# Two convolution feed-forward down projections by seven block products instead of eight

## The reference, cut to what matters

```python
def conv_ffn(h, w_up, conv_w, conv_b, w_down):
    u = h @ w_up                      # 1024 -> 2 * 2816
    # causal depthwise convolution of width 3 along the tokens, + conv_b
    ...
    a, gate = jnp.split(u, 2, axis=-1)
    return (jax.nn.silu(gate) * a) @ w_down   # 2816 -> 1024
...
        x = x + conv_ffn(h, ffn_w_up[layer], ffn_conv_w[layer], ffn_conv_b[layer],
                         ffn_w_down[layer])
```

## Time and profile before

| | us |
|---|---|
| median of 3 runs (3202.98 to 3204.32) | 3203.75 |
| span of the profiled execution | 3201.8 |
| lies around the span, median less span | 1.95 |
| PE busy | 3186.1 |
| DVE busy | 1969.6 |
| ACT busy | 1271.3 |
| POOL busy | 404.6 |

### The profile page before, as it was taken

How to read it: one execution, slowest core, us unless ns; L and a number is a source line. 1 busy time by engine, 2 the same in 40 slices (tenths; PEclk the granted TensorE clock), 3 DMA queues, 4 the chain that set the end, 5 groups by cost and what they waited for, 6 DMA issues and landing times.

```text
span 3201.8 us, 44978 instructions
## 1 busy us (share of the span) xinstructions
PE 3186.1 (100%) x16214; PEld 2672.4 (83%) x16214; DVE 1969.6 (62%) x2804; ACT 1271.3 (40%) x1734; POOL 404.6 (13%) x356
## 2 busy tenths in 40 slices
PE   9999999999999999999999999999999999999998
PEld 7788888889998788888889998768888888888887
DVE  8455567585557455557585555666665744585656
ACT  4433333334453433343334453254332523553423
POOL 2100000124221100000124221051000101320001
PEclk9999999999999999999999999999999999999999
...
GB/s 267 67 167 206 126 94 167 140 92 106 106 99 106 55 169 208 121 98 166 142 87 106 106 99 83 86 21 112 99 99 93 105 99 92 47 85 100 92 99 79
DMA packets 100037, 359.24 MB, mean 112 GB/s; under 512 B 11056, under 2 KB 13360, under 8 KB 99760
## 3 DMA queue, kind: packets, MB, share of 16 engines
...
...
## 4 chain that ended last, share of the span: by engine, by line
PE 94%; DVE 2%; POOLq 1%; issue 1%; ACT 1%; DVEq 1%; DMA 0%; ACTq 0%; SPq 0%; POOL 0%
PE pb L687 21%; PE pb L688 21%; PE pb L689 21%; PE pb L1002 6%; PE pb L719 2%; PE pb L720 2%; PE pb L723 2%; PE pb L759 2%; PE pb L757 2%; PE pb L758 2%; PE pb L1110 1%; PE pb L1485 1%; PE pb L1486 1%; PE pb L1487 1%; PE pb L978 1%
## 5 line engine op out<-in xcount | busy, mean ns | idle before, releaser
L1557 ACT ACTIVATE hi<-raw 128x1024 fp32r<-128x1024 f32 x500 | 524.8, 1056 | 850.0 <-PE pb L689 543.5
L2181 DVE TENSOR_TENSOR lo<-raw,hi 128x1024 fp32r<-128x1024 f32 (+1 forms) x500 | 617.6, 1241 | 330.1 <-ACT hi L1557 304.3
L687 PE MATMUL pb<-yH,hi 128*128 128x512 f32 (+1 forms) x1664 | 644.2, 387 | 0.0
L688 PE MATMUL pb<-yL,hi 128*128 128x512 f32 (+1 forms) x1664 | 644.0, 387 | 0.0
L689 PE MATMUL pb<-yH,lo 128*128 128x512 f32 (+1 forms) x1664 | 643.9, 387 | 0.0
L687 PE MATMUL pb<-hH,hi 128*128 128x512 f32 x1128 | 440.5, 391 | 0.0
L688 PE MATMUL pb<-hL,hi 128*128 128x512 f32 x1128 | 439.0, 389 | 0.0
L689 PE MATMUL pb<-hH,lo 128*128 128x512 f32 x1128 | 438.9, 389 | 0.0
L687 PEld LDWEIGHTS pb<-yH,hi 128*128 128x128 f32 x1664 | 312.5, 188 | 63.6
L689 PEld LDWEIGHTS pb<-yH,lo 128*128 128x128 f32 x1664 | 312.4, 188 | 63.5
L688 PEld LDWEIGHTS pb<-yL,hi 128*128 128x128 f32 x1664 | 312.5, 188 | 63.4
...
## 6 DMA issues: line engine op xcount, KB each, us to landing
...
```

Of the source, the lines that this page charges most:

```text
L687: pe.matmul(out, whi, ahi, start=first, stop=False)
L688: pe.matmul(out, whi, alo, start=False, stop=False)
L1557: act.activation(hi[:, s], raw[:, s], ACT.Copy).then_inc(hi_ready, 1)
L2181: dve.tensor_tensor(lo[:, s, 0:width], raw[:, s, 0:width], hi[:, s, 0:width].bitcast(F32), ALU.subtract).then_inc(lo_ready, 1)
```

## The change

The down projections of the first two slabs of each layer's convolution block, four in all, are done by seven products. A down slab becomes four groups g = 0 to 3 of two output tiles. Each group has 84 matmuls of 256 columns. The inner channels are split into even and odd hidden tiles (the weights are put into that order on the host), the tokens into halves. Products 0 to 6 of hidden tiles are numbered m; the pair (2k, 2k+1) gives four token sums t1 to t4. DVE makes them, ACT rounds them (`middle_hi`), DVE makes remainders (`middle_lo`, event `m_lo`). GpSimd makes the weight sums into a new buffer `ext` (even groups) or `act3` (odd groups), ACT and DVE split them (`down_sum_hi`, `down_sum_lo`, event `e_lo`). Results are added to `x` straight from the banks, in six adds for a group, and counted by `x_part`. Groups 0 and 1 are interleaved: `lead0`, `lead1`, `follow0`, `follow1`, then groups 2 and 3 whole. SP's loads of the tiles behind a group wait for that group's weight sums too. `zT` and `rows` change places, and the scratch for GpSimd's transfers is smaller.

```diff
+FAST_1 = 2 * len(FAST_SLABS) * FAST_GROUPS
+FAST_DOWN = (0, 1)
...
+        d_sum = lambda q: act3[:, 4:7] if q else ext[:, 0:3]
+        d_sumL = lambda q: halved[:, 4:7] if q else extR[:, 0:3]
+        d_sumH = lambda q: tabR[:, 1:4] if q else extR[:, 3:6]
+        d_even = act3[:, 7]
...
+            loaded = early
+            for layer in range(LAYERS):
+                for j in FAST_DOWN:
+                    n = d_tile(layer, j) + RING
+                    into_ring_from(loaded, n)
+                    for g in range(FAST_GROUPS):
+                        sp.wait_ge(w_sums, d_at(layer, j, g) + 1)
+                        into_ring(n + 2 * g)
+                        into_ring(n + 2 * g + 1)
+                    loaded = n + KT
+            into_ring_from(loaded, TILES)
...
+            def down_sums(layer, j, g):
+                e, at = d_sum(g % 2), d_at(layer, j, g)
+                four_sums(d_tile(layer, j) + 2 * g, [e[:, i] for i in range(3)],
+                          5 * (at - 1) + (2 if g == 2 else 0))
...
+                def product_of(out, weights, tokens, first=True, ks=range(4), rest=False):
+                    (wH, wL), (aH, aL) = weights, tokens
+                    for k in ks:
+                        w = slice(k * P, (k + 1) * P)
+                        for n, (wP, aP) in enumerate(((wH, aH), (wH, aL), (wL, aH))):
+                            ins = pe.matmul(out, wP[:, w], aP[:, k], start=first and k == n == 0, stop=k == 3 and n == 2,
+                                            skip_group_check=not first and not rest)
+                    return ins
...
+                def begin():
+                    pe.wait_ge(lo_ready, tiles.next())
+                    pe.wait_ge(bank_free, banks.next(2))
+                    if g == 0:
+                        pe.wait_ge(y_ready, y0 + 7)
+                    product_of(one_sum, own(s0, 0), middle(0, 0)).then_inc(p_full, 1)
+                def with_own_sum():
+                    pe.wait_ge(lo_ready, tiles.next())
+                    if g == 0:
+                        pe.wait_ge(m_lo, t_all - 1)
+                    product_of(other_sum, own(s1, 0), token(1)).then_inc(p_full, 1)
+                def lead():
+                    begin()
+                    with_own_sum()
+                    product_of(upper, own(s0, 1), middle(1, 0), ks=early)
+                    product_of(lower_sum, own(s1, 1), token(4), ks=early)
+                def follow():
+                    ks = range(4)
+                    pe.wait_ge(e_lo, at + 1)
+                    if g == 0:
+                        pe.wait_ge(x_part, 3 * (p0 - FAST_1) + 1)
+                        product_of(one_sum, summed_w(2), token(2), False, early)
+                        pe.wait_ge(y_ready, y0 + KT)
+                        ks = late
+                    product_of(upper, own(s0, 1), middle(1, 0), False, late, True).then_inc(tile_done, 1)
+                    pe.wait_ge(m_lo, t_all)
+                    product_of(lower_sum, own(s1, 1), token(4), False, late, True).then_inc(tile_done, 1)
+                    pe.wait_ge(x_part, 3 * (p0 - FAST_1) + (3 if g else 1))
+                    product_of(one_sum, summed_w(2), token(2), False, ks).then_inc(p_full, 1)
+                    pe.wait_ge(x_part, 3 * (p0 - FAST_1) + (4 if g else 2))
+                    product_of(other_sum, summed_w(4), middle(1, 1), False).then_inc(p_full, 1)
+                    pe.wait_ge(x_part, 3 * (p0 - FAST_1) + (6 if g else 5))
+                    product_of(one_sum, summed_w(3), token(3), False).then_inc(p_full, 1)
+                def whole():
+                    begin()
+                    product_of(upper, own(s0, 1), middle(1, 0)).then_inc(tile_done, 1)
+                    with_own_sum()
+                    if g == 2:
+                        product_of(lower_sum, own(s1, 1), token(4)).then_inc(tile_done, 1)
+                    pe.wait_ge(e_lo, at + 1)
+                    pe.wait_ge(x_part, 3 * (at - FAST_1) + 1)
+                    product_of(one_sum, summed_w(2), token(2), False).then_inc(p_full, 1)
+                    if g == 3:
+                        product_of(lower_sum, own(s1, 1), token(4)).then_inc(tile_done, 1)
+                    pe.wait_ge(x_part, 3 * (at - FAST_1) + 2)
+                    product_of(other_sum, summed_w(4), middle(1, 1), False).then_inc(p_full, 1)
+                    pe.wait_ge(x_part, 3 * (at - FAST_1) + 3)
+                    product_of(one_sum, summed_w(3), token(3), False).then_inc(p_full, 1)
+                return lead, follow, whole
...
+            def fast_down(layer, j, y0):
+                (lead0, follow0, _), (lead1, follow1, _) = (down_group(layer, j, g, y0) for g in (0, 1))
+                lead0()
+                lead1()
+                follow0()
+                follow1()
+                for g in (2, 3):
+                    down_group(layer, j, g, y0)[2]()
...
+                    if j in FAST_DOWN:
+                        fast_down(layer, j, y_k.value())
+                    elif last:
...
+                        if fast and i >= 2 * n - RING:
+                            if i < 2 * n - 1:
+                                down_hi(layer, j, (i - 2 * n + RING) // 2, i % 2)
+                            if i in (2 * n - 3, 2 * n - 2):
+                                down_sum_hi(layer, j, i - 2 * n + 3)
+                        elif i + 1 < 2 * n:
...
+                    if fast:
+                        product_rounded(n - 1)
+                        act.wait_ge(m_last, slab + 1)
+                        middle_hi(3, 1, 4)
+                        for g in (2, 3):
+                            down_hi(layer, j, g, 0)
+                            down_hi(layer, j, g, 1)
+                            down_sum_hi(layer, j, g)
+                        done.next(KT)
+                        for s in (1, 2, 3):
+                            tick(s)
...
+                def one_of():
+                    dve.wait_ge(p_full, p + first)
+                    dve.tensor_tensor(x0[:, TH[0]], X, x0[:, TH[0]], ALU.add).then_inc(x_part, 1)
...
+            def fast_down(layer, j, finish):
+                one0, other0, two0, lower0, upper0, last0 = x_adds(layer, j, 0)
+                one1, other1, two1, lower1, upper1, last1 = x_adds(layer, j, 1)
+                one0()
+                other0()
+                down_lo(layer, j, 1, 1)
+                finish()
+                one1()
+                other1()
+                middle_lo(3, 1, 4, 5 * (d_slab(layer, j) + 1))
+                down_sum_lo(layer, j, 1)
+                two0()
+                lower0()
+                down_lo(layer, j, 2, 0)
+                upper0()
+                last0()
+                two1()
+                lower1()
+                upper1()
+                down_lo(layer, j, 2, 1)
+                last1()
+                one, other, two, lower, upper, last = x_adds(layer, j, 2)
+                one()
+                down_lo(layer, j, 3, 0)
+                other()
+                down_sum_lo(layer, j, 2)
+                lower()
+                two()
+                down_lo(layer, j, 3, 1)
+                upper()
+                last()
+                one, other, two, lower, upper, last = x_adds(layer, j, 3)
+                one()
+                down_sum_lo(layer, j, 3)
+                tick(1)
+                other()
+                two()
+                tick(2)
+                lower()
+                upper()
+                tick(3)
+                last()
...
+                    def first_token_sum(k):
+                        ins = dve.tensor_tensor(d_raw(1, k), d_even[:, TH[1]], d_even[:, TH[0]], ALU.subtract)
+                        if k == 3:
+                            ins.then_inc(m_sums, 1)
+                    def token_sums_of(k, made):
+                        b1, b2 = d_even, A[:, 2]
+                        _, t2, t3, t4 = (d_raw(i, k) for i in (1, 2, 3, 4))
+                        dve.tensor_tensor(t3, b2[:, TH[1]], b1[:, TH[1]], ALU.subtract)
+                        dve.drain()
+                        dve.tensor_tensor(t2, t3, b1[:, TH[0]], ALU.add)
+                        dve.drain()
+                        dve.tensor_tensor(t4, b2[:, TH[0]], t2, ALU.subtract)
+                        dve.drain().then_inc(made, 1)
+                    def remainder(m):
+                        dve.wait_ge(product_hi, ph.next())
+                        dve.tensor_tensor(midL[:, m], product_at(m), midH[:, m].bitcast(F32), ALU.subtract)
+                        dve.drain().then_inc(y_ready, 1)
...
+                        if fast and i == 2 * n - 1:
+                            remainder(m - 1)
+                            middle_lo(3, 0, 1, 5 * slab + 4)
                         drained.next()
                         dve.wait_ge(tile_done, done.next())
                         dve.tensor_tensor(st[:, s], pb[:, s], rows, ALU.mult).then_inc(bank_free, 1)
```

(30 more changed lines are left out.)

154 lines of the change are left out of this document (127 added, 27 removed).

## The result

| | before | after |
|---|---|---|
| median, us | 3203.49 (3202.98 to 3204.32, 4 runs) | 3267.51 (3266.33 to 3268.15, 4 runs) |
| ratio, 95% interval | | 1.0199 (1.0185 to 1.0214) |
| span of the profiled execution | 3201.8 | 3265.9 |

What follows compares the result with a forecast made beforehand. PE's own work was taken as the bound (busy 3186.1 of 3201.8 us). Per slab -3.2 + 4.0 + 1.2 + 1.0 = +3.0, four slabs +12, so a median of some 3216, range 3202 to 3225.

Steps and rivals of the forecast that it cites:

- Term 1: Down slabs on PE: 336 matmuls of 256 columns replace 43.52 us of work, gaining 3.2 a slab, 12.8 for four.
- Term 2: First down matmul: PE waits for product 6's remainder, behind DVE's queue of the second-last up tile, 4.0 us (3.5 to 4.7).
- Rival D: Seam: GpSimd stretches DVE's taps by half, as remainders; first wait 5.0 to 5.5, kernel 3219 to 3227; chance 0.17.
- the token work of the first twelve up tiles: Up tiles ahead of the down stage: DVE's token work fits beside its 4.7 of 5.44 us, at no cost.
- Term 3: Group 2: PE waits for its weight sums, made by GpSimd only after group 0; 1.2 us a slab, bounds 0.9 to 2.4.
- Term 4: After the seam wait: PE's clock falls to half, 1.9 us of work hit, 1.0 lost a slab, bounds 0 to 1.7.
- The rest costs nothing: Down stage: DVE's group work takes 6.9 of 10.1 us, token work fits, loads run ahead; no added time.
- Sum: Per slab: -3.2 + 4.0 + 1.2 + 1.0 = +3.0 us; four slabs +12.
- B: Down slabs: both waits, but clock holds and GpSimd hardly disturbs DVE; +1.2 to +1.9 a slab, 3208 to 3212; chance 0.20.
- C: Seam: DVE isn't late, only the gain from removed matmuls is left, 3191 to 3197; chance 0.11.

Runs made afterwards that it cites:

- the last kernel: Only groups 2 and 3 by seven products, DVE's queue reordered, GpSimd's group 3 sums held back, against the kernel before: 3198.02, ratio 0.9983.

## Why the prediction was right, and where it failed

**Term 1, matmuls removed (12.8): consistent.** Rows show 0.120 from matmul to matmul after too, at the full clock; with this term, the waits and the loss worked out from the granted clock, the sum closes to 1 us, and the last kernel gets 5.3 of the 6.4 that half of it promises.

**Term 2, the wait for product 6 (4.0 a slab): the step that failed.** Place and mechanism were right, with DVE's queue of the second-last up tile read to the instruction: 3.5 forecast with GpSimd idle, 3.4 measured where nothing else disturbs it. Measured in all was 14.6 in a layer's first slab and 10.9 in its second. Two things were missing. First, GpSimd: the prediction took two rows in which remainders took half as much again for a rate, and let it act on few instructions, for 0.5. It is an added wait for the rest of the GpSimd instruction under way, on each DVE instruction with two SBUF inputs that begins in that time: 8.0 and 7.6. The rows already held it: 2.84 less 1.76 and 3.46 less 2.36 are both 1.1, where a rate would have given unequal differences. The first of these rows is one instruction and the second two, of which only one was hit: in the trace the two tiles' remainders take 1.22 and 2.32. Rival D had the place right, the taps suffer too, but it also took a rate, for 1.5 to 2 in place of 8. Second, the first slab: "the token work of the first twelve up tiles fits beside DVE's 4.7 of 5.44" is so for a DVE that starts on time. In a layer's first slab it starts behind PE; before, its shorter tiles had made that good by the eleventh, and with token sums they don't, which costs 3.3 (6.7 less 3.4, without GpSimd).

**Term 3, the second wait (1.2, bounds 0.9 to 2.4): 2.7.** The chain was right and mis-sized for the same reason: group 2's four sums take 6.5 (2314.08 to 2320.54) where 5.8 was forecast, the tile's remainder 1.54 where 1.15, and the sums' remainder 2.48 where 1.7. The lower bound was also added up wrongly: with the hand-overs at nothing the terms make 11.3, less 10.8 is 0.5, not 0.9.

**Term 4, the clock (1.0, bounds 0 to 1.7): 3.3 to 3.8.** The prediction put 1.9 us of work into the low stretch of each slab. Behind the first waits it was 2.9 to 5.5, which costs 2.0 and 1.3 in layer 0. And it didn't ask whether the second wait would bring the clock down again, which it did each time, for 3.4 us of work and a loss of 1.5.

**"The rest costs nothing": right for the waits it named.** No wait for `x_part`, `m_lo` or loads; the token work is the exception, and showed as more of term 2, as the prediction said it would.

**Sum.** A slab: -3.2 + 12.7 + 2.7 + 3.8 = +16.0, four times 64; the 3.8 holds the 3.3 of the granted clock and what stays unexplained. Rivals B and C fell with GpSimd's cost; B's conditions (waits without disturbance) were brought about by leaving out all of GpSimd's sums, and even there the time was 3222, since the clock and the first slab's late start remain.
